# Low weight halves from GpSimd to VectorE, and the prompt's first column tiles inside the sample's router

## The reference

```
h = rmsnorm(x, norm1_g)
proj = h @ w_in                         # 3088 columns: q, k, v, z, x/B/C, dt
att = differential_attention(q, k, v)   # 4 heads, partial rotary on q and k
ssm = bidirectional_ssd(z, xbc, dt)     # centred conv of width 5, silu, two scans
x = x + concat(att, ssm) @ w_out
h = rmsnorm(x, norm2_g)
aff = softmax(h @ w_router); gate, idx = top_k(aff.T, cap)   # each of 16 experts picks tokens
x = x + scatter(expert(h[idx]) * gate)
y = rmsnorm(x, final_g)
```

## Time and profile before

| what | value |
|---|---|
| median of 3 runs | 1988.18 us (1987.91 to 1988.87) |
| the profiled execution | 1986.56 us, span 1984.7 us, mean granted clock 0.976 |
| PE busy | 1854.5 us, 93% |
| DVE busy | 1476.4 us, 74% |
| ACT busy | 1062.3 us, 54% |
| POOL busy | 478.9 us, 24%, of which L597 (36 low halves) 167.8 us, 4662 ns each |
| chain that ended last | PE 78%, DVE 11%, ACT 5% of the span |

### The profile page before, as it was taken

How to read it: one execution, slowest core, us unless ns; L and a number is a source line. 1 busy time by engine, 2 the same in 40 slices (tenths; PEclk the granted TensorE clock), 3 DMA queues, 4 the chain that set the end, 5 groups by cost and what they waited for, 6 DMA issues and landing times.

```text
span 1984.7 us, 31670 instructions
## 1 busy us (share of the span) xinstructions
PE 1854.5 (93%) x11554; PEld 1654.6 (83%) x11554; DVE 1476.4 (74%) x2236; ACT 1062.3 (54%) x1536; POOL 478.9 (24%) x370
## 2 busy tenths in 40 slices
PE   6999988998899989987987999999999999999995
PEld 6887876887679988756777999999999999999994
DVE  5335786887777578977767777787877777877786
ACT  4333337896671433376534555555665555556564
POOL 3434333220860133433410110101111111011120
PEclk9999999999999989999987999999999999999998
DMA  6332321000023423300355777777777777777886
GB/s 206 102 116 101 104 77 43 1 1 1 27 78 141 182 88 109 100 11 12 107 199 183 244 243 238 259 243 263 265 250 255 237 233 253 248 269 251 292 277 241
DMA packets 62755, 325.13 MB, mean 164 GB/s; under 512 B 8336, under 2 KB 14608, under 8 KB 32464
## 3 DMA queue, kind: packets, MB, share of 16 engines
q1 hardware_dynamic: 46640, 265.55, 37.7%
q0 software_dynamic: 16032, 58.47, 10.1%
HBM read 287.55 MB, written 34.87 MB: 162 GB/s over the span
## 4 chain that ended last, share of the span: by engine, by line
PE 78%; DVE 11%; ACT 5%; issue 4%; POOL 1%; DMA 1%; SPq 0%; POOLq 0%; ACTq 0%; DVEq 0%
PE psum L2417 20%; PE psum L1992 10%; PE psum L1993 9%; PE psum L1994 9%; PE psum L2418 9%; PE psum L2440 3%; PE psum L2439 3%; DVE conv_acc L1436 3%; PE psum L2143 3%; PE psum L2122 2%; PE psum L2131 1%; PE psum L2123 1%; PE psum L2204 1%; PE psum L2271 1%; ACT prob L990 1%
## 5 line engine op out<-in xcount | busy, mean ns | idle before, releaser
L2417 PE MATMUL psum<-xT,whi 128*128 128x384 f32 x1024 | 295.4, 361 | 1.2 <-DVE xT L1968 1.2
L2417 PE MATMUL psum<-xT,whi_x 128*128 128x384 f32 x1024 | 293.7, 359 | 0.0
L1897 DVE TENSOR_TENSOR wlo_x<-wraw_x,whi_x 128x2048 fp32r<-128x2048 f32 x96 | 218.4, 2287 | 58.9 <-ACT whi_x L1212 58.9
L2418 PE MATMUL psum<-xT,wlo 128*128 128x192 f32 x1024 | 257.2, 251 | 0.0
L2418 PE MATMUL psum<-xT,wlo_x 128*128 128x192 f32 x1024 | 256.4, 250 | 0.0
L1992 PE MATMUL psum<-ht_hi,whi 128*128 128x512 f32 (+1 forms) x624 | 238.2, 382 | 19.4 <-POOL wlo L597 7.0
L1993 PE MATMUL psum<-ht_lo,whi 128*128 128x512 f32 (+1 forms) x624 | 235.7, 378 | 0.0
L1994 PE MATMUL psum<-ht_hi,wlo 128*128 128x512 f32 (+1 forms) x624 | 235.5, 377 | 0.0
L1897 DVE TENSOR_TENSOR wlo<-wraw,whi 128x2048 fp32r<-128x2048 f32 x94 | 213.4, 2283 | 16.2 <-ACT whi L1212 16.2
L597 POOL TENSOR_TENSOR wlo<-wraw,whi 128x2048 fp32r<-128x2048 f32 x36 | 167.8, 4662 | 220.3 <-ACT whi L830 220.3
L2418 PEld LDWEIGHTS psum<-xT,wlo 128*128 128x128 f32 x1024 | 196.7, 192 | 0.6
(11 more groups left out here) (379 smaller groups left out, 4299.2 us busy)
## 6 DMA issues: line engine op xcount, KB each, us to landing
wraw<-moe_chunks SPq DMA_DIRECT2D x96, 1024.0 KB, 5.2
wraw_x<-moe_chunks SPq DMA_DIRECT2D x96, 1024.0 KB, 6.3
wraw<-w_in_chunks SPq DMA_DIRECT2D x36, 1024.0 KB, 4.9
wraw<-w_out_chunks SPq DMA_DIRECT2D x8, 1024.0 KB, 6.1
xin<-x POOLq DMA_DIRECT2D x12, 512.0 KB, 5.4
acc_scratch<-x POOLq DMA_DIRECT2D x12, 512.0 KB, 3.2
h_scratch<-h POOLq DMA_DIRECT2D x12, 512.0 KB, 4.1
fin<-acc_scratch SPq DMA_DIRECT2D x11, 512.0 KB, 10.6
```

The lines of the kernel that those rows point to most:

```text
L1897: tt(moe_lo[i % 4], moe_raw[i % 4].rearrange("p (k n) -> p k n", k=KT), moe_hi[i % 4].bitcast(F32), ALU.subtract).then_inc(w_lo_done, 1)
L2417: mm(bank[:, 0:2 * TOK], hi[:, k, cols], xT[:, k, :], start=(k == 0), stop=False)
L2418: last = mm(bank[:, 0:TOK], lo[:, k, cols], xT[:, k, 0:TOK], start=False, stop=(k == KT - 1))
```

## The change

It makes two changes of place. First, POOL's 36 low weight halves go to DVE, at the head of each odd slot (`split`, L1271, the same instruction that DVE already uses for a few chunks). POOL keeps only transfers in the projection, and its wait for these halves ahead of attention goes. Second, PE turns token tiles 8 and 9 inside stage 5, between the router's transposes of tiles 6 and 7, into banks 0 to 3; ACT and DVE split them there; PE does the early halves of block 2's column tiles 0 and 1 behind the last router product; POOL loads tiles 10 and 11 behind the last row store; ACT and DVE norm them in stage 6; PE turns them at the start of block 2. The transposed affinities move from bank 2 to bank 5.

```diff
         def turn_bank(t, q):
-            return pb[(6, 4)[t % 2] + q]
+            return pb[(6, 4)[t % 2] + q] if t not in (8, 9) else pb[2 * (t - 8) + q]
...
                     for at_, m in enumerate(ORDER):
-                        if at_ % 2 == 0 and at_ < 24:
-                            g = FIRST_CHUNK[b] + at_ // 2 + 1
-                            pool.wait_ge(w_hi_done, g + 1)
-                            pool.tensor_tensor(wlo[:, g % 2, :, :],
-                                               wraw[:, g % 2, :].rearrange("p (k n) -> p k n", k=KT),
-                                               whi[:, g % 2, :, :].bitcast(F32), ALU.subtract
-                                               ).then_inc(w_lo_done, 1)
...
-                pool.wait_ge(w_lo_done, FIRST_OUT_CHUNK[s] + 1)
...
+                if s == 0:
+                    load_tile(10)
+                    load_tile(11)
                 for i in range(4):
                     pool.wait_ge(rows_out[i], 32 * (t0 + nt) // 4)
...
-                if s == 0:
-                    load_tile(10)
-                    load_tile(11)
...
-                        rms(10)
-                        rms(11)
                         tokens_hi(10)
                         tokens_hi(11)
...
+                    if s == 0 and i == nt:
+                        act.wait_ge(op_done, 4 * nt)
+                        tokens_hi(8)
+                        tokens_hi(9)
                 end()
...
                 if s == 0:
-                    act.wait_ge(op_done, 4 * nt)
-                    tokens_hi(8)
-                    tokens_hi(9)
+                    rms(10)
+                    rms(11)
...
-                    if b == 2:
-                        normed(10)
-                        normed(11)
...
                     for at_, m in enumerate(ORDER):
+                        if at_ % 2 and at_ < 24:
+                            split(FIRST_CHUNK[b] + at_ // 2 + 1)
...
+                if s == 0:
+                    tokens_lo(8)
+                    tokens_lo(9)
                 dve.wait_ge(lg_done, t0 + nt)
                 end()
...
+                if s == 0:
+                    normed(10)
+                    normed(11)
                 dve.wait_ge(rt_p, 2 * s + 1)
-                own.link(dve.tensor_copy(affT[:, 0:L // 2], pb[2][0:64, 0:L // 2]))
+                own.link(dve.tensor_copy(affT[:, 0:L // 2], pb[5][0:64, 0:L // 2]))
                 if s == 0:
-                    tokens_lo(8)
-                    tokens_lo(9)
                     end()
...
+                    elif b == 2:
+                        turn_tokens(10)
+                        phase(pe, ph)
+                        turn_tokens(11)
...
+                    if s == 0 and i == nt:
+                        pe.wait_ge(part_out, 12 * nt)
+                        turn_tokens(8)
+                        turn_tokens(9)
...
+                if s == 0:
+                    pe.wait_ge(w_lo_done, FIRST_CHUNK[2] + 1)
+                    pe.wait_ge(ht_lo_done, token_step(9, 1))
+                    projection_column(2, 0, slice(0, BLK // 2))
+                    projection_column(2, 1, slice(0, BLK // 2))
                 phase(pe, ph + 6)
-                if s == 0:
-                    turn_tokens(8)
-                pe.wait_ge(rt_v, 2 * s + 1)
-                if s == 0:
-                    turn_tokens(9)
                 pe.wait_ge(rt_v, 2 * s + 2)
```

More of the change, by code:

```diff
@@ L2002, in turn_tokens @@
                     pe.wait_ge(rot_out, NR - 1)
-                if t == 9:
-                    pe.wait_ge(rot_out, NR * 2)
                 for q in range(2):
@@ L2010, in turn_tokens, with projection_column @@
                     last.then_inc(h_turned, 1)
+            def projection_column(b, m, toks, ks=range(KT)):
+                bank = tile_bank(b, m)
+                if m == DT:
+                    for k in ks:
+                        mm(bank[0:32, :], w_dt[:, k, :], ht_hi[:, k, :], start=(k == 0), stop=False)
+                        last = mm(bank[0:32, :], w_dt[:, k, :], ht_lo[:, k, :], start=False, stop=(k == KT - 1))
+                    return last
+                g = FIRST_CHUNK[b] + m // 2
+                cols = slice(m % 2 * P, m % 2 * P + P)
+                for k in ks:
+                    last = split3(bank[:, toks], whi[:, g % 2, k, cols], wlo[:, g % 2, k, cols],
+                                  ht_hi[:, k, toks], ht_lo[:, k, toks], k == 0, k == KT - 1)
+                return last
             for s, (t0, nt, blocks, cap) in enumerate(SEQS):
@@ L2014, in _ @@
                 L = nt * P
-                if s:
-                    phase(pe, ph)
                 for b in blocks:
                     def column_tile(m, toks, ks=range(KT)):
-                        bank = tile_bank(b, m)
-                        if m == DT:
-                            for k in ks:
-                                mm(bank[0:32, :], w_dt[:, k, :], ht_hi[:, k, :], start=(k == 0), stop=False)
-                                last = mm(bank[0:32, :], w_dt[:, k, :], ht_lo[:, k, :], start=False, stop=(k == KT - 1))
-                            return last
-                        g = FIRST_CHUNK[b] + m // 2
-                        cols = slice(m % 2 * P, m % 2 * P + P)
-                        for k in ks:
-                            last = split3(bank[:, toks], whi[:, g % 2, k, cols], wlo[:, g % 2, k, cols],
-                                          ht_hi[:, k, toks], ht_lo[:, k, toks], k == 0, k == KT - 1)
-                        return last
+                        return projection_column(b, m, toks, ks)
                     early, late = slice(0, BLK // 2), slice(BLK // 2, BLK)
@@ L2049, in _ @@
                         column_tile(1, early, second)
+                    elif b == 2:
+                        turn_tokens(10)
+                        phase(pe, ph)
+                        turn_tokens(11)
                     else:
-                        pe.wait_ge(ht_lo_done, 2 * (TPB * b + 2))
+                        pe.wait_ge(ht_lo_done, 4)
                         column_tile(0, early)
-                        turn_tokens(TPB * b + 2)
-                        if b == 0:
-                            turn_tokens(3)
+                        turn_tokens(2)
+                        turn_tokens(3)
                         column_tile(1, early)
-                        if b:
-                            turn_tokens(TPB * b + 3)
                     pe.wait_ge(ht_lo_done, 2 * TPB * (b + 1))
@@ L2361, in _ @@
                         last.then_inc(lg_done, 1)
-                phase(pe, ph + 6)
-                if s == 0:
-                    turn_tokens(8)
-                pe.wait_ge(rt_v, 2 * s + 1)
-                if s == 0:
-                    turn_tokens(9)
+                if s == 0:
[3 more added lines that the diff above has]
+                    projection_column(2, 1, slice(0, BLK // 2))
+                phase(pe, ph + 6)
                 pe.wait_ge(rt_v, 2 * s + 2)
                 for i in range(nt // 2):
-                    last = pe.transpose(pb[2][0:64, i * P:(i + 1) * P], aff[:, i].rearrange("p h n -> p (h n)"), ident)
+                    last = pe.transpose(pb[5][0:64, i * P:(i + 1) * P], aff[:, i].rearrange("p h n -> p (h n)"), ident)
                 last.then_inc(rt_p, 1)
```

## The result

The changed kernel's median is 1969.63 us (1969.1 to 1970.79, four runs) against 1988.05 (1986.75 to 1988.87): ratio 0.9906 [0.9894, 0.9918]. Two later sets on other chips gave 0.9920 [0.9902, 0.9937] and 0.9913 [0.9900, 0.9927], medians 1970.32 and 1969.95. It is faster, as forecast; the gain is 16 to 19 us where 13.7 was forecast. One execution of all that follow, of the low halves alone, took 4588 us, more than twice the others, and is left out of its ratio.

A forecast was written before the change was run, and what follows sets the result against it. TensorE, 93% busy, was taken as the bound. The terms -3.7, -3.4, +3.0, -2.8 and -6.8 sum to -13.7 us, so 1988.2 becomes 1974.5 us; range 1970 to 1979, forecast's chance 53%.

The forecast's parts named there:

- rival 4: Blocks 1 and 2: the 5.5 us step is the convolution's own, so the kernel gets slower, 2001 us; chance 4%.
- join: Join of blocks 0 and 1: token tile 7's load goes out 5.6 us earlier; -2.8 us, bounds 0 and -2.96.
- block 1: Copy of tile 8 to start of tile 20: 7.4 us lost before; -3.7 us, bounds 0 and -7.4.
- router part: Sample's router to block 2: moved turns and early halves cover VectorE's softmax; -6.8 us, bounds 0 and -8.2.
- T: Start of block 2's first late half, 718.28 before; forecast 711.5, with one short spell at 1.2 GHz.
- block 2's head: VectorE's first low half there comes behind two rounds of choice, so PE waits; +3 us, bounds 0 and +5.
- block 2, copy of tile 8 to D: Block 2 from tile 8's copy on: 4.9 us lost before, perhaps two late low halves remain; -3.4 us, bounds 0 and -4.9.
- three come late: 3 x 1.2 = 3.7 us: Block 1: first VectorE low half just in time, three late, each costing PE about 1.2 us, 3.7 us together.
- Rival 1: Router to block 2: the clock stays low through the early halves, the router change gives nothing, 1981 us; chance 11%.
- rival 2: Router to block 2: clock at 2.4 GHz throughout, first late half at 710.1, time 1973.1 us; chance 19%.
- Rivals 3 and 5: 3: low halves later than counted, 1981 us, 10%. 5: something after block 2 takes the gain back, within 0.2%, 3%.
- differences carry over unchanged: Whole kernel: times come from one profiled execution of 1986.56 us, 1.6 us under the timed median; differences were assumed to hold.

The follow-up runs named there:

- pool_reads: Changed kernel plus a two-operand POOL subtraction at the former low halves' moments in block 2; a VectorE step of 0.75 us lasts 3.97 us, no whole time given.
- the third column: Changed kernel with block 2's second low half and third tile's early half in the router, tokens 10 and 11 turned before the affinities: 0.9931, 1974.40 us.

## Where the prediction held, and which of its sizes failed

**Direction and mechanism** held. POOL's low half holds VectorE's two-operand steps (pool_reads); taking it away shortens the pair to 12.01 us (12.10 forecast); rival 4 is excluded. The sizes did not add up: -18.4 us in the first set against -13.7, below the low end of 1970. Term by term, mean of the profiled executions of changed against before:

| term | forecast | measured |
|---|---|---|
| join (first product to the copy of block 1's tile 8, so with block 0) | -2.8 | -3.2 |
| block 1 (copy of tile 8 to the start of tile 20) | -3.7 | -4.5 |
| router part (B to T) | -6.8 | -7.4 |
| block 2's head (T to its third tile) | +3.0 | +2.7 |
| block 2, third tile to the copy of tile 8 | 0 | +1.2 |
| block 2, copy of tile 8 to D | -3.4 | -3.9 |
| start of the program to the first product | 0 | -0.4 |

**The step that failed is block 1's "three come late: 3 x 1.2 = 3.7 us".** Three did come late, and from 243.47 to 255.48 the pair takes PE 12.01 us where its products need 10.88, 1.13 lost, as forecast. But the pair that ends at 267.49 also holds the first turns of a finished value tile, 0.60 us of PE's time at 266.52, for which the working had already set time aside in its 61.2 us; of that wait 0.37 us is left. From the copy of tile 8 to the start of tile 20 block 1 took 68.60 us before and takes 64.09 (64.16 and 64.12 in the other two traces): it gives 4.5 of the 7.4 lost us and keeps 2.9, where 3.7 each was forecast.

```profile
215.24 0.60 ACT L951 ACTIVATE stage<-psum 128x512 f32<-128x512 f32 x1 [2.00 <-PE psum L1990]
```
```profile
266.52 0.60 PE L2068 MATMUL psum<-cst,stage 128*128 128x128 f32 x4
...
279.33 0.48 PE L1988 MATMUL psum<-ht_hi,whi 128*128 128x512 f32 x1
```

The join, the router and block 2 behind its tile 8 gave 0.4 to 0.6 us more each as well, so the sum to D is -15.4. For the join the prediction's own working gives the whole idle time: 163.1 lies ahead of 163.44, where PE's own work ends, which is -2.96 and not -2.8.

**Block 2's head** was right: from T to the third tile 8.55 to 8.59 us in all three executions against 5.85 before (718.28 to 724.13), +2.7 where +3.0 was forecast. That the first profile shows a wait of 1.06 us only is the clock: its late halves ran at 0.57 from 704 to 708 and used up the rest. In the other two traces of the changed kernel, with the wait at full length, a low spell followed it (0.64 from 712 to 715 in one, 0.52 from 710 to 713 in the other), and from the third tile to the copy of tile 8 they took 1.7 us longer than the 38.31 of before; the first took 0.1 longer.

**The router part** was right within its scatter: 51.01 to 51.07 us in every execution with it, 57.66 and 59.13 in the two of the kernel before, -6.6 against the profile that the forecast used, -7.4 against both. T itself comes out at 711.7 on the old axis (702.72, and the 8.97 us by which B came earlier), forecast 711.5. That is in part luck, since its reason was only partly right: the low spell was there, at the place forecast, but the working started T's path at the landing of token tile 10. In the trace its square follows ACT's exponential of 691.88 without idle time, at 701.2 on the old axis where 700 was taken, and that exponential waited, over VectorE, for the router's last products, which end at 690.96.

```profile
691.88 0.42 ACT L1139 ACTIVATE aff<-aff 128x256 f32<-128x256 f32 x1 [5.44 <-DVE aff L1774]
692.21 1.04 ACT L828 ACTIVATE junk<-xin 128x1024 bf16<-128x1024 f32 x1
```

Rival 1 is out; rival 2 (T at 710.1 on the old axis, 8.2 us less) is out too, since PE ran at 0.61 and 0.52 from 686 to 694. Rivals 3 and 5 find nothing in the table: no low half came later than counted, and what is gained at D is still there at S within the 7 us by which that stage scatters.

**From -15.4 to -18.4.** The second step that failed is "differences carry over unchanged": the forecast took one execution of before, put the scatter between executions at nothing, and made its range of bounds of the terms alone. All 15 executions of the changed kernel on record have a mean of 1971.1 us, the 84 of the kernel before 1987.65: -16.5, near the -16.0 to which the stages up to S add up in the traces, and 1971.1 lies inside the range of 1970 to 1979. The four of the first set lie at 1969.1 to 1970.79, so some 1.5 us of their gain is the favourable end of that scatter, and 0.4 is the median of before, 1988.05. Which of the untouched stages gave it is not shown, since the first set has one trace of the changed kernel.

## What to carry to other kernels

Where VectorE sets the pace, ask what POOL reads at the same time: a step can cost VectorE more when POOL does it (4.2 us lost a pair) than when VectorE does it itself (2.28 us). Work moved into a stage where its engine waits pays only until the next late resource, so look behind the removed wait before counting it; here the third column gained nothing until VectorE's order behind it was changed as well. Compare changes of under 1% stage by stage in more than one execution, since the whole time also holds stages that vary from execution to execution with unchanged code, and put their scatter into the range of a forecast.

## What was not expected of the hardware

- Fills on POOL did not hold two-operand steps (all 32 convolution steps of block 2 stayed at 0.75 us), but they lengthened one-operand ones: the sine step, 0.49 us in the changed kernel, took 1.53 us under a fill, and one of the convolution's first steps, under the fills of 741.72 to 745.41, 1.77 instead of 0.48.

```profile
705.00 1.53 DVE L1370 TENSOR_SCALAR sin_t<-sin_t,lamt 128x512 f32<-128x512 f32 x1
...
743.92 1.77 DVE L1430 TENSOR_SCALAR conv_acc<-xbc,par 128x512 f32<-128x512 f32 x1
```

- The same router code, with PE counted busy through its products, ran at 2.4 GHz in one execution of the kernel before and at 1.2 in the next (3.69 and 6.85 us for 32 products); no change in the kernel is needed for a difference of 4.3 us.
